# Output projection of an encoder layer by token halves, the first half normed while the second is projected

## The reference

```python
mix = jnp.concatenate([o_h, o_c], axis=-1) @ w_out[l]
h = h + g1[:, None, :] * mix                       # h1 of the kernel
hn2 = _modulate(_rmsnorm(h, norm_ffn_g[l]), sh2, sc2)
ffn = _peer(hn2, peer_wq[l], peer_keys1[l], peer_keys2[l], peer_u[l], peer_v[l])
...
q = (h @ wq).reshape(nb, L, PEER_HEADS, PEER_DKEY)     # in _peer, then scores against the keys
v1, i1 = lax.top_k(s1, PEER_TOPK)
```

## Time and profile before

| | us |
|---|---|
| median of 3 runs | 2950.88 |
| lowest, highest | 2946.54, 2953.84 |
| span of the profiled execution (its page gives no other time of its own) | 2964.7 |
| TensorE busy in the span | 2795.0 (94%) |
| VectorE | 2245.3 (76%) |
| GpSimd | 1259.1 (42%) |
| ScalarE | 865.7 (29%) |

### The profile page before, as it was taken

The page is one execution under the profiler, slowest core; times in us unless marked ns, Lnnn a source line. Parts: engine busy times, 40 slices in busy tenths (PEclk is TensorE's granted clock), DMA queues, the critical chain, the costliest instruction groups (busy, mean ns, idle before and its releaser), DMA issues.

```text
span 2964.7 us, 31179 instructions
## 1 busy us (share of the span) xinstructions
PE 2795.0 (94%) x10124; PEld 1518.3 (51%) x10124; DVE 2245.3 (76%) x4581; ACT 865.7 (29%) x1715; POOL 1259.1 (42%) x1091
## 2 busy tenths in 40 slices
PE   6999889888999998999999989999999999999995
PEld 3677677667754444544554544544444444444442
DVE  5898666327789999999898967776777677767775
ACT  3223554222211114664664756820000000000004
POOL 1001111223254444444444444464566566556651
PEclk8999999999999999999999989999999999999998
DMA  5641111133499999999999998999999999999994
GB/s 202 248 171 43 44 36 68 68 121 100 135 406 381 383 375 343 393 377 377 386 355 377 367 396 321 417 408 400 401 404 403 408 395 394 406 406 399 404 389 191
DMA packets 282610, 911.47 MB, mean 307 GB/s; under 512 B 25808, under 2 KB 73168, under 8 KB 275152
## 3 DMA queue, kind: packets, MB, share of 16 engines
q0 software_dynamic: 147456, 536.94, 46.6%
q1 hardware_dynamic: 97648, 297.56, 26.7%
q10 hardware_dynamic: 37344, 74.98, 6.6%
HBM read 826.01 MB, written 83.36 MB: 307 GB/s over the span
## 4 chain that ended last, share of the span: by engine, by line
PE 31%; DMA 20%; DVE 10%; POOL 8%; issue 3%; ACT 2%; DVEq 1%; another core or an unknown queue 1%; SPq 0%; ACTq 0%; PEldq 0%; POOLq 0%
PE s_pu L1651 22%; DMA s_slot<-in_v,s_row 17%; POOL s_slot L1599 8%; DVE s_slot L2110 5%; PE s_pw L1688 3%; PE s_ps L1698 2%; DVE s_hB L2124 2%; DMA s_slot<-in_u,s_row 1%; DMA s_wr<-s_w 1%; PE s_pu L340 1%; PE s_pu L344 1%; PE s_pu L341 1%; DVEq L2145 1%; ACT s_hotw L1856 1%
## 5 line engine op out<-in xcount | busy, mean ns | idle before, releaser
L1651 PE MATMUL s_pu<-s_hn,s_ut 128*128 128x512 f32 x2304 | 1012.9, 596 | 5.4 <-ACT s_gst L1803 3.9
L1599 POOL DMA_INDIRECT s_slot<-in_v,s_row x512 | 620.4, 1212 | 390.3 <-DVE s_hB L2124 277.6
L2124 DVE SCALAR_TENSOR_TENSOR s_hB<-s_slot,s_dot,s_hB 128x1024 f32<-128x1024 f32 x469 | 593.9, 1284 | 248.9 <-DMA s_slot<-in_v,s_row 232.6
L1599 POOL DMA_INDIRECT s_slot<-in_u,s_row x512 | 504.0, 984 | 619.5 <-DVE s_slot L2110 510.3
L1651 PEld LDWEIGHTS s_pu<-s_hn,s_ut 128*128 128x128 f32 x2304 | 435.4, 191 | 536.4 <-issue 535.1
L2110 DVE SCALAR_TENSOR_TENSOR s_slot<-s_slot,s_ps 128x1024 f32<-128x1024 f32 x512 | 607.7, 1219 | 60.8 <-DMA s_slot<-in_u,s_row 32.3
L1755 PE MATMUL s_ps<-s_ct,s_vt 128*128 128x512 f32 x1024 | 460.3, 592 | 0.0
L1755 PEld LDWEIGHTS s_ps<-s_ct,s_vt 128*128 128x128 f32 x1024 | 194.6, 190 | 245.4 <-issue 245.4
L1856 ACT ACTIVATE s_hotw<-s_hot,s_rest 128x128 bf16<-128x128 bf16 x1024 | 308.5, 423 | 27.2 <-ACT s_gst L1803 21.7
L1933 ACT ACTIVATE s_sq<-y 128x512 f32<-128x512 f32 x16 | 8.9, 626 | 919.0 <-DVE y L2196 918.9
L1755 PE MATMUL s_pw<-s_ct,s_vt 128*128 128x512 f32 x512 | 248.1, 608 | 22.3 <-DMA s_vt<-in_v_tiles 22.3
(11 more groups left out here) (315 smaller groups left out, 2769.0 us busy)
## 6 DMA issues: line engine op xcount, KB each, us to landing
s_ut<-in_u_tiles SPq DMA_DIRECT2D x128, 512.0 KB
s_vt<-in_v_tiles SPq DMA_DIRECT2D x32, 2048.0 KB
s_g<-s_gst ACTq DMA_DIRECT2D x120, 256.0 KB
s_w<-s_wb ACTq DMA_DIRECT2D x15, 2048.0 KB
s_wr<-s_w SPq DMA_DIRECT2D x16, 1920.0 KB
s_gr<-s_g SPq DMA_DIRECT2D x60, 512.0 KB, 27.4
s_ada<-in_ada SPq DMA_DIRECT2D x48, 512.0 KB, 6.2
s2w_raw<-in_w_in SPq DMA_DIRECT2D x26, 512.0 KB, 4.0
```

The lines of the kernel that those rows point to most:

```text
L1599: pool.indirect_dma_start(out=slot[s][:, :], out_offset=None, in_=io[kind], in_offset=bass.IndirectOffsetOnAxis(ap=row[b][:, j:j + 1], axi ...
L1651: mm = pe.matmul(pu[:, n % 2, :], ut[n % UR][:, k, :], hn[:, k, :], start=(k == 0), stop=(k == DC - 1))
L2124: dve.scalar_tensor_tensor(y, s, dot[b][:, j:j + 1], y, ALU.mult, ALU.add).then_inc(taken, 1)
```

## The change

The six tiles that `step4` projects become 12 items of one tile and one half: `ITEMS` lists tiles 2 to 7 of half 0, then tiles 2 to 7 of half 1. As each tile's weights are used twice, all split weights are kept: five hi/lo pairs in SBUF of their own (`out_hi`, `out_lo`) and the two slots of `m.w_hi`, `m.w_lo` for the query weights. Residual, square and the running sum of squares go by item, with four buffers of 512 columns for x and squares in place of two of 1024. Sums and root exist per half. Half 0's follow item 6 (tile 2 of half 1), and its y, hi and lo are made between the residuals of items 7 to 10. Half 1's sums are put behind slice 3 of the query projection. Half 1 gets no hi and lo here: h1 of it and its root stay in SBUF, and `step6` makes `hn` in f32, one slice a round, with VectorE (scale x root) and ScalarE (shift). The two GpSimd adds and two waits for them go. Three buffers of `step6` move to make room. `m.h1` in HBM holds the same as before.

```diff
-    h1 = at("s4_h1", [P, DC, T], F32, F0)
+    h1 = at("s4_h1", [P, 2, DC, HALF], F32, F0)
+    ITEMS = [(k, h) for h in range(2) for k in range(2, DC)]
+    LAST = (5, 11)
...
+        def parts(j):
+            return (out_hi[j], out_lo[j]) if j < 5 else (m.w_hi[j - 5], m.w_lo[j - 5])
+        def raw(j):
+            return m.next_w[(j + 1) % 2]
...
         def _(sp):
+            def load_w(j):
+                if j >= 2:
+                    sp.wait_ge(split, j - 1)
...
+            load_w(1)
+            for i, (k, h) in enumerate(ITEMS):
+                sp.wait_ge(h1_ready, 1 if i < 2 else 2 if i < 4 else i - 1)
+                sp.dma_start(x[:, i % 4, :], io["xT"][k][:, h * HALF:(h + 1) * HALF]).then_inc(x_in[i % 4], 16)
+                if 3 <= i < 8:
+                    load_w(i - 1)
+            for k in range(2):
+                sp.dma_start(two(m.h1[k]), h1[:, :, k, :]).then_inc(stored, 16)
+            for i, (k, h) in enumerate(ITEMS):
+                sp.wait_ge(h1_ready, i + 3)
+                sp.dma_start(m.h1[k][:, h * HALF:(h + 1) * HALF], h1[:, h, k, :]).then_inc(stored, 16)
...
         def _(act):
+            round_tile(0)
+            square_pair(0)
+            square_pair(1)
+            for i in range(6):
+                round_tile(i + 1)
+                square(i)
+            square(6)
+            root_of(0)
+            for i, ks in ((7, (0, 1, 2)), (8, (3, 4)), (9, (5, 6)), (10, (7,)), (11, ())):
+                for k in ks:
+                    shifted(k)
+                square(i)
+            root_of(1)
...
         def _(pe):
+            def tile_half(i):
+                k, h = ITEMS[i]
+                if k > 2:
+                    pe.wait_ge(split, k - 2)
+                pe.wait_ge(h1_ready, i + 1)
+                hi, lo = m.second if k == 2 else parts(k - 3)
+                project(pe, ps[k % 2], hi, lo, m.hn_hi, m.hn_lo, halves=(h,)).then_inc(summed, 1)
...
+            for i in range(len(ITEMS)):
+                tile_half(i)
+                if i == 6:
+                    square_sums(0)
+            pe.wait_ge(split, 7)
             for k in range(DC):
                 pe.wait_ge(y_lo, k + 1)
                 for s in range(2):
...
+                if k == 3:
+                    square_sums(1)
             pe.drain()
...
         def _(dve):
+            for i in range(6):
+                residual(i)
+                if i:
+                    add_square(i - 1)
+            dve.sem_inc(sq_summed, 1)
+            residual(6)
+            add_square(6)
+            dve.wait_ge(root, 1)
+            for ys, los, i in (((0, 1, 2), (0,), 7), ((3, 4), (1, 2), 8), ((5, 6), (3, 4), 9), ((7,), (5, 6, 7), 10)):
+                for k in ys:
+                    normed(k)
+                for k in los:
+                    remainder(k)
+                if i > 7:
+                    add_square(i - 1)
+                residual(i)
+            add_square(10)
+            dve.sem_inc(sq_summed, 1)
+            residual(11)
@@ step6 @@
-                if h <= 2:
-                    ks = slice((h - 1) * DC // 2, h * DC // 2)
-                    pool.tensor_tensor(hn[:, ks, :], m.hn_hi[:, 1, ks, :].bitcast(F32), m.hn_lo[:, 1, ks, :].bitcast(F32),
-                                       ALU.add).then_inc(hn_ready, 1)
...
-            pe.wait_ge(hn_ready, 2)
+            pe.wait_ge(hn_ready, DC)
...
+                act.wait_ge(xn_made, h + 1)
+                act.activation(hn[:, h, :], hn[:, h, :], ACT.Identity, bias=m.mods[:, 3, h:h + 1]).then_inc(hn_ready, 1)
...
+                    if not s:
+                        dve.scalar_tensor_tensor(hn[:, h, :], m.h1_half[:, 1, h, :], m.mods[:, 4, h:h + 1], m.r[:, 1, :],
+                                                 ALU.mult, ALU.mult).then_inc(xn_made, 1)
```

More of the change, by code:

```diff
@@ L1148, in step4 @@
         ps_q = [m.pu[:, s, :] for s in range(2)]
[L1149 to L1153, removed]
+        ps_ss = ctx.enter_context(nc.psum_tensor("s4_ss", [P, 2, HALF], F32))
@@ L1154, in step4 @@
+        x_in = [sem(f"s4_x_in{s}") for s in range(4)]
+        w_in = [sem(f"s4_w_in{s}") for s in range(2)]
+        rounded, split = sem("s4_rounded"), sem("s4_split")
+        summed, h1_ready, sq_ready, sq_used, sq_summed = (sem(f"s4_{n}") for n in ("sum", "h1r", "sqr", "squ", "sqs"))
+        ss_ready, root = [sem(f"s4_ss_r{h}") for h in range(2)], sem("s4_root")
+        xn_ready, y_hi, y_lo, stored = (sem(f"s4_{n}") for n in ("xn", "yhi", "ylo", "st"))
         block = ctx.enter_context(nc.Block())
+        def parts(j):
+            return (out_hi[j], out_lo[j]) if j < 5 else (m.w_hi[j - 5], m.w_lo[j - 5])
@@ L1180, in _, with round_tile @@
[L1180 to L1184, removed]
-                act.wait_ge(xn_ready, k + 1)
-                act.activation(m.hn_hi[:, :, k, :], two(y[:, k, :]), ACT.Identity, bias=m.mods[:, 3, k:k + 1])\
-                   .then_inc(y_hi, 1)
+            def round_tile(j):
+                if j:
+                    act.wait_ge(w_in[(j + 1) % 2], 16 * ((j + 1) // 2))
+                act.activation(parts(j)[0][:, :, :], raw(j)[:, :, :], ACT.Copy).then_inc(rounded, 1)
@@ L1194, in _ @@
         @block.tensor
         def _(pe):
[L1196 to L1207, removed]
@@ L1257, in _ @@
-            for k in range(DC - 2, DC):
-                remainder(k)
+                dve.scalar_tensor_tensor(m.hn_lo[:, 0, k, :], y[:, k, :], m.mods[:, 3, k:k + 1],
+                                         m.hn_hi[:, 0, k, :].bitcast(F32), ALU.add, ALU.subtract).then_inc(y_lo, 1)
+            for k in range(2):
+                dve.scalar_tensor_tensor(h1[:, :, k, :], two(ps[k][:, :]), m.mods[:, 2, k:k + 1], x[:, 2 * k:2 * k + 2, :],
+                                         ALU.mult, ALU.add).then_inc(h1_ready, 1)
```

114 lines of the change are left out of this document (56 added, 58 removed).

## The result

The changed kernel took 2932.4 us, the median of five runs (2922.57 to 2934.55), beside 2946.54 for the kernel before in the same series (five runs, 2942.56 to 2953.84). The two medians lie 14.1 us apart. The ratio on record, which isn't that of the medians (0.9952), is 0.9937 with an interval of 0.992 to 0.9954: 18.6 us of 2946.54, between 13.6 and 23.6. The forecast was 16.1 us less, 2934.8 us. In a second series the same pair gave 0.9939 (0.9916 to 0.9962), with medians 14.7 us apart.

The account below looks back on a forecast made before the run. TensorE was taken as the bound except for 31.2 us between the last projection matmul and the step's end, paced by VectorE's norm passes. Saving 16.6 less 0.5 gives 16.1 us, 2950.9 to 2934.8 us, range 2930 to 2940.

Parts of the forecast that it names:

- the stretch behind the first gather: From the first gather to the end of the span: the same 2156 us as before, within 5.
- the start of the block: Output projection by halves on TensorE, slow first matmuls included: last item ends at 653.4 as now, value taken 0.
- The step: Output and query projection: after the last projection matmul 31.2 us become 14.6, saving 16.6; first item to end about 81.7 us.
- The root: Gathering half's root on ScalarE: ready 4.7 us after the end of item 6 on TensorE.
- The last round: Last scores round: the dense half's added VectorE pass costs 0.5 us, bounds 0 to 1.8.
- The bounds: Range of the 16.1 us saving: 14.3 with a stretch of 1.8, 17.1 with no last-round cost and less barrier.
- Weights: Weight feed for half-tile items in the output projection: ready with 4.4 us of slack, cost 0.
- GpSimd against VectorE: Weight remainders on GpSimd in the step: by SBUF contention with VectorE none would come under 3.47 us.
- A: A norm or weight is late inside the twelve items, so TensorE pays; 8 us gone, 2943 us; chance 0.06.
- B: The step is shorter but gathers and tiles behind it end where they did; 2950 us; chance 0.07.
- C: Weight feed doesn't overlap, a tile costs 10.2 us against 5.44; slower, 2958.6 us; chance 0.04.
- D: y_lo still comes after the last item, query matmuls wait for hn_lo; saves 10.2, 2940.7 us; chance 0.05.

Follow-up runs that it names:

- e4_width: Kernel before, whole tiles in old order, but norm passes in the step only for the gathering half, dense half in f32 in scores rounds: 2955.92 us, ratio 0.9976.
- e1_after: The changed kernel run again with no edit, against the kernel before: 2947.66 us, ratio 0.9939.
- e5_late: Changed kernel with the gathering half's y, hi and lo passes put behind the last residual, sums and root still early: 2948.29 us in one run.
- e3_ahead: Changed kernel with round 2's query weights loaded and split in the step and the last round's dense-half slice made in the first: 2940.19 us, ratio 0.9919.
- e6_pool2: Changed kernel with each GpSimd weight remainder of the step made twice: 2939.11 us in one run.
- e7_pool4: Changed kernel with each GpSimd weight remainder of the step made four times: 2952.53 us in one run.
- e2_pad: Changed kernel with nine needless half tiles on TensorE ahead of the step's barrier: 2990.21 us, ratio 1.0094 to the kernel before.

## Why the prediction was right, and where not

The mechanism that I forecast is the one that the runs show. Two terms that the prediction left at nothing were not nothing, and they are the steps that failed.

- **What failed, first: the stretch behind the first gather.** "The same 2156 us from there to the end, within 5": the first trace has 2137.1, 18.9 us less, so the span came out at 2926.1 and not at 2948.6. The step of the reasoning at fault is that one span was taken as a constant of code that the change hardly touches, and that what is saved in one span was taken off a median of three other runs. Over nine traces that stretch is 2137.1 to 2158.0 us, and 2155.5 in the changed kernel's second trace; a spread larger than the whole effect lay in a term that had no row of its own. The timed runs spread as far: 2946.80 to 2972.45 us over 18 runs of the kernel before.
- **What failed, second: the start of the block.** "Value taken: 0" for the output projection, with the last item at 653.4 "as now". The wait ahead of the first item was 4.69 us before (4.65 in `e4_width`, which keeps that part) and 2.99 to 3.05 in every trace with halves: 1.7 us saved that the sum hasn't got. The twelve semaphore increments at the head of TensorE's list went with the change, and the releaser of VectorE's first pass moved from them to the barrier; that they are the cause is read from the traces, and no run took them out alone. The slow first matmuls, kept in the forecast "as now", were missing in four traces, another 1.6 us. From TensorE's last matmul ahead of the block to the first gather it is 227.1 us before, 209.5 in the first trace and 207.3 in `e1_after`: 17.6 and 19.7 us saved, where the forecast was 16.1.
- **The time.** 2934.8 us was forecast and 2932.4 measured, but that this is so near is partly luck. The forecast started from 2950.88, the median of three runs; with two more it is 2946.54. The saving is 14.1 us by the medians and 18.6 by the ratio (13.6 to 23.6), and both 16.1 and the traces' 17.6 to 19.7 lie within that. The timing can't tell them apart.
- **The step.** Forecast: 98.3 becomes 81.7, no idle over 1 us in it. Measured in the like trace: 81.62, no idle at all. The twelve items ran at the pace I took from the scores loop (5.44 us), the sums cost 3.7, and 48 query matmuls 10.9. The experiments divide the 16.7 us, if their parts add up: 4.6 come with the width alone (`e4_width`), 5.5 with the norm beside the projection (`e5_late` against the changed kernel), and the other 6.6, by subtraction, with the early sums and root and the half-wide items. No run has these last alone.
- **The root** came 5.6 us after item 6, not 4.7. The term missed a table load ahead of the Ln. The slack took it: the last `hn_lo` is there at 644.05, 7.3 us early.
- **The last round.** Forecast +0.5 us, bounds 0 to 1.8. From the last round's first copy (783.19 before, 763.02 afterwards) to the first gather it is 25.48 us before and 25.97 to 26.00 in the six traces by halves that keep the pass (all but `e3_ahead`): 0.5 us, as forecast. Over a longer stretch, from the last query matmul to the first gather, it can't be seen: 124.05 before, and 123.82 to 125.38 in these six.
- **The bounds.** 14.3 was worked out wrongly: 16.6 - 1.8 is 14.8, and the 0.5 us was charged twice. Nor were "all slacks above" over 4 us: the second root's was 2.7.
- **Weights.** Forecast: 4.4 us of slack, nothing paid. `e6_pool2` pays nothing for 2.4 us more, `e7_pool4` pays at 7.2 us more.
- **GpSimd against VectorE.** I wrote that by the rule in the Trainium skill, GPSIMD Engine Reference, section 8 (Key points), no remainder of the step would come under 3.47 us. That fell: in the changed kernel five of the seven take 2.38 us. The rule names contention with VectorE instructions of two SBUF inputs, and the trace agrees with it: no VectorE pass at all falls beside these five, and where one with two SBUF inputs does, it shows. What failed was my step from the rule to this block, since a sum of squares no longer starts with each remainder. The changed kernel's GpSimd in the step and in a scores round, where the new pass of the dense half (687.07, 0.74 us) runs beside it:

```profile
592.37 2.38 POOL L1237 TENSOR_TENSOR s_out_lo<-s_next_w,s_out_hi 128x1024 fp32r<-128x1024 f32 x1 [4.04 <-ACT s_out_hi L1195]
...
687.19 2.89 POOL L328 TENSOR_TENSOR w_lo<-s5w_raw,w_hi 128x1024 fp32r<-128x1024 f32 x1 [3.05 <-ACT w_hi L324]
```

- **Rivals.** A: no item waits, and the weights have slack left (`e6_pool2`). B: refuted by `e2_pad` as far as the end stays unchanged; that a few us are given back isn't excluded. C: appears only when each remainder is made four times. D: its mark is absent, and `e5_late` shows what it would have looked like.

What stays open: why the stretch behind the first gather varies by 21 us between executions. The traces place it some 900 to 1000 us behind the first gather, and no run here was made for its cause.

## What to carry to other kernels

When an engine-wide barrier ends a step, the time between the bounding engine's last full work and that barrier is paid nearly in full (42.5 to 46 of 49 us in `e2_pad`); look for a part of the dependent work that can be finished for one half of the data while the other half still feeds that engine, and check each producer's cycle against the shorter item. Compare traces by distances between events inside the changed stretch, and not by spans: the step here is 79.99 us in three traces whose start of TensorE is alike, while whole spans of one kernel differ by 20 us. Start the measure at the last event that the change can't touch: from the first matmul, 1.7 us of this change drop out of sight. Removing the wait is worth more than its length where TensorE drops to its lower clock behind it.

## What the hardware showed that I had not expected

- **A short wait can cost TensorE more than itself.** After 3.58 us of waiting in `e5_late` the matmuls start 0.43 us apart and not 0.23, and the granted clock of the stretch is 0.80:

```profile
650.00:658.00 8.00, 4.42 (x13) 3.23 (x12) 7.09 (x11) 4.46 (x7) 0.00 (x0) 0.80 0.09 33
```

  So the wait cost 5.5 us for 3.58. In `e4_width` it was 13.8 us for 10.9 us of work behind a wait of 6.50, and at the start of the step it was 1.6 us (the first trace against `e1_after`). It isn't so each time: both of these waited 3.0 us ahead of the first item, and only one had slow matmuls behind it. The two spacings are near a factor of two, as are the two levels of the clock, 1.2 and 2.4 GHz.
- **A GpSimd pass can hold a VectorE pass for nearly three times its length.** VectorE's sum of squares over [128, 1024] takes 1.22 us. In `e6_pool2` it starts 0.02 us behind a remainder and lasts until that and a part of the next are over:

```profile
581.59 3.47 DVE L1299 TENSOR_TENSOR s_sq_sum<-s_sq 128x1024 f32<-128x1024 f32 x1 [1.21 <-ACT s_sq L1199]
```

```profile
581.57 2.40 POOL L1240 TENSOR_TENSOR s_out_lo<-s_next_w,s_out_hi 128x1024 fp32r<-128x1024 f32 x1
583.93 3.38 POOL L1238 TENSOR_TENSOR s_out_lo<-s_next_w,s_out_hi 128x1024 fp32r<-128x1024 f32 x1
```

  VectorE ends at 585.06: it waits out the first pass and then runs its own 1.1 us, by which the second pass is longer (3.38 against 2.4). In the kernel before, where the two start together too, VectorE took its 1.22 us and the remainder 3.47, against 2.39 at the least; there VectorE had started 0.01 us ahead (600.28 against 600.29). So the size of a stretch is about what is left of the other engine's pass, and in these pairs the one that started later paid. The scores round above fits: VectorE starts at 687.07 and takes its 0.74 us, GpSimd starts at 687.19 and takes 0.5 us more than 2.38.
